# Feed-forward's first half: three blocks take turns over the first norm's operand tiles where two did

## The reference, cut to what matters

```python
x = layer_norm(DEEPNORM_ALPHA * x + g1 * mix, ln1_g[l], ln1_b[l])
h = x * (1.0 + sc2) + sh2
f = jnp.square(jax.nn.relu(h @ w_m1[l] + b_m1[l])) @ w_m2[l] + b_m2[l]
x = layer_norm(DEEPNORM_ALPHA * x + g2 * f, ln2_g[l], ln2_b[l])
```

## Time and profile before

| what | value |
|---|---|
| time, median of 3 runs | 2608.17 us (2605.45 to 2609.82) |
| time of the profiled execution | 2609.6 us |
| its span | 2607.8 us |
| mean granted TensorE clock in it | 0.981 |
| PE, DVE, ACT, POOL busy | 96%, 77%, 53%, 32% |

### The profile page before, as it was taken

How to read it: one execution, slowest core, us unless ns; L and a number is a source line. 1 busy time by engine, 2 the same in 40 slices (tenths; PEclk the granted TensorE clock), 3 DMA queues, 4 the chain that set the end, 5 groups by cost and what they waited for, 6 DMA issues and landing times.

```text
span 2607.8 us, 42659 instructions
## 1 busy us (share of the span) xinstructions
PE 2510.8 (96%) x16524; PEld 2291.1 (88%) x16524; DVE 2014.3 (77%) x2606; ACT 1379.2 (53%) x2169; POOL 830.3 (32%) x765
## 2 busy tenths in 40 slices
PE   6799999999998999999999989999999999999989
PEld 3688888889987888888888879999889999999978
DVE  7889888878889785555555679898868888889855
ACT  0344445444455454445544477776656666666643
POOL 0100011002244520001111239986104666666630
PEclk9799999999999999999999999999999999999989
DMA  9988776787865886556555534445455444444434
GB/s 351 348 298 271 263 251 221 252 278 253 291 227 190 283 280 207 190 178 200 190 192 191 189 122 162 156 159 166 162 164 174 149 152 154 159 157 155 156 111 146
DMA packets 147010, 534.35 MB, mean 205 GB/s; under 512 B 16855, under 2 KB 17016, under 8 KB 146424
## 3 DMA queue, kind: packets, MB, share of 16 engines
q1 hardware_dynamic: 143480, 519.56, 59.6%
q0 software_dynamic: 3328, 12.06, 1.4%
HBM read 525.26 MB, written 6.29 MB: 204 GB/s over the span
## 4 chain that ended last, share of the span: by engine, by line
PE 85%; DVE 7%; issue 3%; DMA 2%; POOL 2%; ACT 1%; SPq 0%; POOLq 0%; DVEq 0%; ACTq 0%
PE ps L610 32%; PE ps L614 26%; PE ps L612 10%; PE ps L613 10%; PE ps L1000 2%; DVE misc L1084 2%; PE ps L672 1%; DMA AF<-in_w_ada 1%; DVE wl L1063 1%; POOL misc L2473 1%; PE ps L701 1%; PE ps L901 1%; PE ps L650 1%; PE ps L732 1%; DMA ring<-in_w_in 1%
## 5 line engine op out<-in xcount | busy, mean ns | idle before, releaser
L1063 DVE TENSOR_TENSOR wl<-ring,wh 128x1024 fp32r<-128x1024 f32 x784 | 1034.5, 1332 | 352.5 <-ACT wh L1819 351.2
L614 PE MATMUL ps<-A,wl 128*128 128x256 f32 x4480 | 1262.2, 282 | 0.0
L1819 ACT CAST wh<-ring 128x1024 fp32r<-128x1024 f32 x784 | 816.0, 1045 | 381.2 <-PE ps L614 361.3
L614 PEld LDWEIGHTS ps<-A,wl 128*128 128x128 f32 x4480 | 855.7, 191 | 0.2
L610 PE MATMUL ps<-A,wh 128*128 128x512 f32 x2176 | 772.2, 399 | 21.3 <-DVE A L1067 7.7
L612 PE MATMUL ps<-A,wh 128*128 128x256 f32 x2304 | 672.8, 292 | 10.3 <-DVE A L1067 9.6
L613 PE MATMUL ps<-A,wh 128*128 128x256 f32 x2304 | 652.6, 283 | 0.0
L610 PE MATMUL ps<-B,wh 128*128 128x512 f32 x1792 | 636.2, 400 | 10.0 <-issue 4.5
L610 PEld LDWEIGHTS ps<-A,wh 128*128 128x128 f32 x2176 | 412.1, 189 | 120.2 <-DVE wl L1063 8.4
L614 PE MATMUL ps<-B,wl 128*128 128x256 f32 x1792 | 501.7, 280 | 0.0
L612 PEld LDWEIGHTS ps<-A,wh 128*128 128x128 f32 x2304 | 442.5, 192 | 12.9 <-issue 10.0
(11 more groups left out here) (253 smaller groups left out, 2245.6 us busy)
## 6 DMA issues: line engine op xcount, KB each, us to landing
ring<-in_w_m SPq DMA_DIRECT2D x256, 512.0 KB, 4.5
ring<-in_hgrn_w_in SPq DMA_DIRECT2D x160, 512.0 KB, 3.8
ring<-in_w_ada SPq DMA_DIRECT2D x146, 512.0 KB, 5.3
ring<-in_w_in SPq DMA_DIRECT2D x144, 512.0 KB, 5.5
ring<-in_conv_w_in SPq DMA_DIRECT2D x96, 512.0 KB, 3.9
AF<-in_w_ada SPq DMA_DIRECT2D x46, 512.0 KB, 8.6
ring<-in_w_ab SPq DMA_DIRECT2D x32, 512.0 KB, 5.9
ring<-in_w_o SPq DMA_DIRECT2D x32, 512.0 KB, 5.7
```

Source lines behind the costliest of these rows:

```text
L614: return e.matmul(dst[:, 0:256], lo, x[:, 0, :], start=False, stop=last)
L1063: e.tensor_tensor(low[:], ring[SLOT[h]][:], hi[:].bitcast(F32), ALU.subtract).then_inc(s.lo, 1)
L1819: e.copy(wh[h % NSPLIT][:], ring[SLOT[h]][:]).then_inc(s.hi, 1)
```

## The change

In the first pass (`fh == 0`) three blocks share the operand tiles. `HALVES` is reordered so that halves 0, 1, 2 are tiles 0 to 7 of blocks 0, 1, 2 and halves 3, 4, 5 their tiles 8 to 15. On PE, tiles 0 to 7 go in turns over the three blocks; then come tiles 8 to 11 of block 0, tiles 8 to 11 of block 1, then tile 12 for blocks 0 and 1 and tile 8 of block 2, and so on, and at the end tiles 12 to 15 of block 2. Halves 4 and 5 are now split among the operand tiles: `hi(4)` and `hi(5)` behind ACT's `high(10)` and `high(11)`, `lo(4)` and `lo(5)` behind DVE's scalings 11 and 12. Behind block n's eviction come halves 6, 7, 8 for n = 0, 1, 2 and then the same two as before. The second pass, the second norm and all else stay.

```diff
-    HALVES += by_turns("w_m1", [32 * _i + n for n in range(32)])
+    HALVES += by_turns("w_m1", [32 * _i + n for n in range(32)], 2 + (_i == 0))
...
+def split_behind_three(n):
+    return (n + 6,) if n < 3 else (2 * n + 3, 2 * n + 4)
+
+THIRD = [(b, k) for b in range(2) for k in range(8, 12)]
+THIRD += [x for k in range(12, 16) for x in ((0, k), (1, k), (2, k - 4))] + [(2, k) for k in range(12, 16)]
...
-            pbs = [bank()[:] for n in range(2)]
-            for part in range(2):
-                halves_by_turns(H_M1[fh] + 2 * part, pbs, lambda k: wait_lo(w, 8 * part + k, 1),
-                           part == 0, part == 1)
-            for n in range(2, 32):
+            pbs = [bank()[:] for n in range(3 if fh == 0 else 2)]
+            if fh == 0:
+                halves_by_turns(H_M1[0], pbs, lambda k: wait_lo(w, k, 1), True, False)
+                for b, k in THIRD:
+                    h = H_M1[0] + 3 + b
+                    wait_lo(w, k, 1)
+                    w.wait_ge(s.lo, h + 1)
+                    done = k_tile(pbs[b], wh[h % NSPLIT][:, k - 8, :], wl[h % NSPLIT][:, k - 8, :], A2[:, :, k, :],
+                                  False, k == 15)
+                    if k == 15:
+                        done.then_inc(s.mm, 1)
+            else:
...
+            for n in range(len(pbs), 32):
...
                 if i == 3:
                     lo((H_M1[0], H_CV)[norm] + 3)
+                if norm == 0 and i in (11, 12):
+                    lo(H_M1[0] + i - 7)
...
-                for j in split_behind(n):
-                    if fh or j > 3:
-                        lo(H_M1[fh] + j)
+                for j in split_behind(n) if fh else split_behind_three(n):
+                    lo(H_M1[fh] + j)
...
-        operand(gp, 1, lambda i: None)
+        def third_block(i):
+            if i in (10, 11):
+                hi(H_M1[0] + i - 6)
+
+        operand(gp, 1, third_block)
...
-                w.wait_ge(s.mm, H_M1[fh] + in_step(n))
+                for j in split_behind(n) if fh else split_behind_three(n):
+                    hi(H_M1[fh] + j)
+                w.wait_ge(s.mm, H_M1[fh] + in_step(n, 2 if fh else 3))
```

More of the change, by code:

```diff
@@ L866, in tensor_program @@
         for fh in range(2):
-            pbs = [bank()[:] for n in range(2)]
-            for part in range(2):
-                halves_by_turns(H_M1[fh] + 2 * part, pbs, lambda k: wait_lo(w, 8 * part + k, 1),
-                           part == 0, part == 1)
-            for n in range(2, 32):
+            pbs = [bank()[:] for n in range(3 if fh == 0 else 2)]
[10 more added lines that the diff above has]
+            else:
+                for part in range(2):
+                    halves_by_turns(H_M1[1] + 2 * part, pbs, lambda k: wait_lo(w, 8 * part + k, 1),
+                                    part == 0, part == 1)
+            for n in range(len(pbs), 32):
                 pb = bank()[:]
@@ L2060, in scalar_program @@
                 pb = bank()[:, 256:512]
-                for j in split_behind(n):
-                    if fh or j > 3:
-                        hi(H_M1[fh] + j)
-                w.wait_ge(s.mm, H_M1[fh] + in_step(n))
+                for j in split_behind(n) if fh else split_behind_three(n):
+                    hi(H_M1[fh] + j)
+                w.wait_ge(s.mm, H_M1[fh] + in_step(n, 2 if fh else 3))
                 w.wait_ge(s.blo, 21 + 32 * fh + n - 3)
```

## The result

| | kernel before | changed kernel |
|---|---|---|
| median (runs) | 2607.72 us (20) | 2611.80 us (20) |
| lowest to highest | 2603.03 to 2609.82 | 2607.45 to 2620.22 |
| ratio, 95% interval | | 1.0019 (1.0012 to 1.0026) |
| span of the profiled execution | 2607.8 | 2608.1 |

The changed kernel is slower by 0.19%, 4.9 us with an interval of 3.1 to 6.8. +5.2 was forecast. The medians themselves lie 4.1 apart: 2613.4 was forecast for this table's 2611.80.

The account below looks back on a forecast made before the run. PE, busy 96% of the span, was taken as the bound, waiting for DVE's operand tiles ahead of block 3. Terms 1.97 + 2.0 + 1.3 = 5.3, say +5.2 us, gave 2613.4 us, range 2607.3 to 2617.3.

Parts of the forecast that it names:

- The wait at tile 11: PE idles some 5.6 us before block 0's tile 11, its low part delayed 4.4 us by `lo(4)`, `lo(5)` on DVE.
- Block 3's start at full clock: With 21 steps left behind the wait, block 3 starts at 817.39 where it started at 815.42: +1.97 us.
- The clock: Behind PE's wait the clock is slow for 4.3 us: +2.0 us, bounds 1.6 and 2.35.
- The short turns: Behind block 0, three turns with one `lo` each make PE wait 0.4 and 0.9 us at halves 8 and 9: +1.3.
- The transfer of half 9: SP issues it behind block 0's chunk; it lands 0.7 us before `hi(9)` wants it and costs nothing.
- Rival (c): Half 9's transfer takes 6.8 us and lands late, with the clock slow for 5.13: +6.3 us, 2614.5; chance 0.14.
- The sum: Likeliest case, 1.97 + 2.0 + 1.3 = 5.3, say +5.2 us, median 2613.4 us; chance 0.63.
- Rival (a): The change works: PE finds tile 11 ready, DVE's two waits under about 1 us together; -1.2 us, 2607.0; chance 0.10.
- Rival (b): PE's wait is there but the clock holds: 1.97 + 1.3 = +3.3 us, 2611.5; chance 0.13.
- Rival (d): The short turns behind block 0 cost nothing: +3.9 us, 2612.1; counted inside the likeliest case.
- the best case: PE finds tile 11 ready and the third block fills the gaps; no case gives over 1.2 us.

Follow-up runs that it names:

- a2_after: The changed kernel run once more, with nothing altered; ratio to the kernel before 1.0017 (1.0009 to 1.0026).
- e4_clock: Changed kernel plus 20 matmuls on ready data in PE's gap ahead of block 0's tile 11; ran once, block 3 at 25.50 us from the restart, no ratio.
- e6_late: Changed kernel with half 4 subtracted behind scaling 13, half 5 split behind the last operand tile, block 2's steps 8 to 15 behind blocks 0 and 1; ratio to before 1.0007.
- e8_block: Changed kernel with halves 4 and 5 split behind the last operand tile and tiles 8 to 15 block by block; block 3 at 24.00 us, no ratio.
- e9_both: `e6_late` with the casts of halves 7 to 12 ahead of the casts to B of blocks 0 to 3; ratio to the kernel before 0.9998 (0.9989 to 1.0006).

## Why the prediction was right

**The wait at tile 11** was right in place and cause. DVE waited 1.13 and 1.91 us where 0.86 and 2.0 were worked out; the first is longer because `hi(4)` waited 0.26 for PE's step on tile 7, which I had 0.4 ahead of it. That step came late because the slow clock behind the restart lasted for two steps more than in the profile before, which I had copied. In `a2_after` it didn't, and the wait was 0.77. PE started again 18.32 from the restart, and 17.96 in `a2_after`; the forecast was 18.02. Block 3's start at full clock, +1.97, follows from the 21 steps that were left: `e4_clock`, with the clock up, has 25.50 against 23.58, +1.9.

**The clock** was sized at 2.0 us, with bounds of 1.6 and 2.35, from 4.3 us at half clock; it was 5.3 in the first execution. Changed kernel against `e4_clock` it is 28.17 - 25.50 = 2.7, and in the second execution 27.37 - 25.50 = 1.9. Of the 2.7, 2.3 is the slow steps and 0.35 is that PE started tile 11 later in that execution. Right within its bounds.

**The short turns** were sized at 1.3: from block 3's start to half 9 it took 9.79 and 9.76 us against 8.44 and 8.48 before, so 1.3. The waits came at halves 8 and 9 as said, split more evenly (0.49 and 0.53 listed, against 0.4 and 0.9).

**The transfer of half 9** was to be hidden with 0.7 us to spare. ACT's cast of half 9 in the changed kernel began behind the cast to B and not behind a transfer, so it was: issued at 817.49, the transfers of this stretch landed 5.2 us later, 1.4 ahead of the cast at 824.11. In `e6_late`, where that cast is wanted earlier, it was 0.69 late. Rival (c) is a real mechanism and didn't bind here.

**The sum**, 5.2 (the terms add up to 5.3), stands against 5.1 to 6.1 at half 9 (37.13 - 32.06 and 37.96 - 31.89) and 4.9 (3.1 to 6.8) in the timed runs. Rival (a) fell: DVE's waits were 3.0 together and not under 1. Rival (b) fell, since the clock went down in both executions. Rival (d) fell, since the short turns cost 1.3. That the sum meets the measured 4.9 within 0.3 us is luck: the interval is 3.7 us wide, and two executions of the same kernel differ by 0.8 at block 3 and by 3.0 from the restart to the end. The places, the order and the sizes of the terms are what was right. I had 0.44 for slower by over 0.2% and 0.52 for within; 0.19% is as near to the line as the sum was.

What I did not see: no version of the third block was worth anything in the timed runs, with its waits repaired too. I gave it 1.2 us in the best case. `e6_late` won 1.5 at block 3 in its one trace, but in three of the four versions whose waits in this stretch had come down to about a microsecond the clock still fell, at a price of the same size.

## What to carry to other kernels

Before an extra operation is put in an in-order queue, write down what the engine it waits for is itself waiting for. Here DVE waited for ACT's cast, which stood behind a tile that waited for DVE, and one line moved up in ACT's program took 2.6 us or more off. If one engine feeds the busiest one tile by tile, work that has no hurry belongs behind the tiles that have, and the busiest engine's own order should put what is ready ahead of what is late.

## What the runs showed of the hardware that was not expected

**Two paces at full clock.** Steps of 512 + 256 columns start every 0.347 us or every 0.353 us, with the clock granted at 1.00 in both. One pace holds for hundreds of steps and changes only at a disturbance. From 840 to 900 the first execution of the kernel before had 0.3466 and its second 0.3534; `e6_late`, `e8_block` and `e9_both` had 0.347 too, the nine others 0.353. The changed kernel had 0.347 from block 3 to its wait for half 8 and 0.353 behind it. Over the 248 steps from block 3 to the middle of block 18 the kernel before took 87.8 us in one execution and 89.3 in the other. These 1.5 us are more than some edits here are worth, and they stand in no wait. What sets it is open.

**Short waits can bring the clock down.** Waits of 1.05 and 0.77 us, of 0.77 and 1.27, and of 1.06 and 0.52 were each followed by slow steps. Waits of 0.75 and 0.52 were not, nor were the kernel before's 0.59 and 0.40 in two executions. Block 3 came 0.8 to 1.5 us later than worked out each time that it happened. The pairs that were followed by slow steps are the longer ones in sum, so this need not be chance; no run varied their length alone.
